# Two feed-forward norms of a two-block float32 kernel: 1/rms applied as a row on VectorE instead of a diagonal on TensorE

## What is computed

```python
# first block
x = x + gate1 * rmsnorm(y, g_post_mix[l])
h = rmsnorm(x, g_pre_ffn[l]) * (1.0 + scale2) + shift2      # "norm1"
gu = h @ w_ffn_in[l]
...
# second block
x = x + ... @ w_out[i]
h = rms_norm(x, norm_ffn_w[i])                                # "norm3"
u = causal_depthwise_conv(h @ w_ffn_up[i], ...)
...
x = x + g * (p[i] @ w_ple_proj[i])                            # p's projection
```

## Time and profile before

| what | us |
|---|---|
| median of three runs | 2794.21 (2787.49 to 2797.47) |
| the profiled execution, its own time | 2796.14 |
| its span in the trace | 2794.4 |
| TensorE busy | 2725.7 (98% of the span) |
| VectorE busy | 1820.3 (65%) |
| ScalarE busy | 1290.2 (46%) |
| GpSimd busy | 290.6 (10%) |
| mean granted TensorE clock | 0.991 of full |

### The profile page before, as it was taken

How to read it: one execution, slowest core, us unless ns; L and a number is a source line. 1 busy time by engine, 2 the same in 40 slices (tenths; PEclk the granted TensorE clock), 3 DMA queues, 4 the chain that set the end, 5 groups by cost and what they waited for, 6 DMA issues and landing times.

```text
span 2794.4 us, 38988 instructions
## 1 busy us (share of the span) xinstructions
PE 2725.7 (98%) x14835; PEld 2346.2 (84%) x14835; DVE 1820.3 (65%) x2017; ACT 1290.2 (46%) x1555; POOL 290.6 (10%) x161
## 2 busy tenths in 40 slices
PE   4899999999999999999999999999999999999998
PEld 4798888788888888888888989878888888888887
DVE  7966779689955556655567544656666654666555
ACT  2256554334444444444444444535555533555454
POOL 3010122100000100000100000100113110131100
PEclk8899999999999999999999999999999999999999
DMA  9975646698935567755566654445555565555553
GB/s 373 353 258 195 224 152 215 227 326 305 340 127 193 180 203 249 254 181 188 187 222 244 216 166 151 161 145 180 182 185 190 180 201 190 192 184 194 182 199 131
DMA packets 299522, 588.70 MB, mean 211 GB/s; under 512 B 12282, under 2 KB 19438, under 8 KB 298510
## 3 DMA queue, kind: packets, MB, share of 16 engines
q1 hardware_dynamic: 292816, 577.84, 61.0%
q10 hardware_dynamic: 6590, 9.27, 1.0%
HBM read 584.98 MB, written 2.10 MB: 210 GB/s over the span
## 4 chain that ended last, share of the span: by engine, by line
PE 89%; DVE 7%; issue 2%; ACT 1%; DMA 1%; SPq 0%; POOL 0%; DVEq 0%; POOLq 0%; ACTq 0%
PE psum L781 13%; PE psum L785 13%; PE psum L783 13%; PE bank L974 12%; PE psum L974 12%; PE bank L977 6%; PE psum L977 6%; PE psum L792 2%; PE psum L796 2%; PE psum L794 2%; DVE ada_acc L865 2%; DVE mod_acc L652 2%; DVE w_lo L739 2%; PE bank L2647 1%; PE bank L947 1%
## 5 line engine op out<-in xcount | busy, mean ns | idle before, releaser
L739 DVE TENSOR_TENSOR w_lo<-raw,w_hi 128x1024 fp32r<-128x1024 f32 x912 | 1165.3, 1293 | 836.7 <-ACT w_hi L727 825.7
L727 ACT ACTIVATE w_hi<-raw 128x1024 fp32r<-128x1024 f32 x912 | 953.6, 1054 | 1269.4 <-PE psum L785 568.4
L974 PE MATMUL psum<-h_both,w_hi 128*128 128x512 f32 x1408 | 495.1, 395 | 0.8 <-DVE x L2415 0.7
L974 PE MATMUL bank<-h_both,w_hi 128*128 128x512 f32 x1408 | 493.8, 395 | 0.0
L977 PE MATMUL bank<-h_both,w_lo 128*128 128x256 f32 x1408 | 394.8, 280 | 0.0
L977 PE MATMUL psum<-h_both,w_lo 128*128 128x256 f32 x1408 | 394.8, 280 | 0.0
L781 PE MATMUL psum<-w_hi,h_both 128*128 128x512 f32 x880 | 348.6, 396 | 0.8 <-ACT tokbuf L1826 0.7
L785 PE MATMUL psum<-w_hi,h_both 128*128 128x512 f32 x880 | 343.5, 390 | 0.0
L783 PE MATMUL psum<-w_lo,h_both 128*128 128x512 f32 x880 | 343.4, 390 | 0.0
L974 PEld LDWEIGHTS psum<-h_both,w_hi 128*128 128x128 f32 x1408 | 264.0, 187 | 62.7 <-DVE x L2415 1.0
L974 PEld LDWEIGHTS bank<-h_both,w_hi 128*128 128x128 f32 x1408 | 263.9, 187 | 61.9
(11 more groups left out here) (369 smaller groups left out, 3188.5 us busy)
## 6 DMA issues: line engine op xcount, KB each, us to landing
raw<-in_w_in_dram SPq DMA_DIRECT2D x120, 1024.0 KB, 5.2
raw<-in_w_ffn_in_dram SPq DMA_DIRECT2D x88, 1024.0 KB, 5.0
raw<-in_w_ffn_up_dram SPq DMA_DIRECT2D x88, 1024.0 KB, 5.0
raw<-in_w_ada_dram SPq DMA_DIRECT2D x64, 1024.0 KB, 5.2
raw<-in_w_ffn_out_dram SPq DMA_DIRECT2D x44, 1024.0 KB, 5.2
raw<-in_w_ffn_down_dram SPq DMA_DIRECT2D x44, 1024.0 KB, 5.1
ada_raw<-in_w_ada_dram SPq DMA_DIRECT2D x64, 512.0 KB, 8.0
raw<-in_w_out_dram SPq DMA_DIRECT2D x32, 1024.0 KB, 5.3
```

Source lines behind the costliest of these rows:

```text
L727: nc.scalar.activation(w_hi[:, slot, :, 0:ncol], raw[:, rs, 2 * h:2 * h + 2, 0:ncol], ACT.Copy).then_inc(split_hi, inc)
L739: nc.vector.tensor_tensor(w_lo[:, slot, :, 0:ncol], raw[:, rs, 2 * h:2 * h + 2, 0:ncol], w_hi[:, slot, :, 0:ncol].bitcast(F32), ALU.subtra ...
L974: pe.matmul(region[:, f, :].rearrange("p (s t) -> p s t", s=2), w_hi[:, slot, kk, cols_], h_both[:, :, k, :], start=first, stop=False, ski ...
```

## The change

1. `normed_dve` is no longer called in norm1, norm2 and norm3. A new `r_row_pe` waits for `rms` itself and multiplies the 1/rms column of `stats` (broadcast along its free axis as the stationary operand) with the identity; the result, a row of 1/rms on all partitions, lies in bank 3 (norm1, norm3) or bank 0 (norm2). VectorE copies it to `r_row`.
2. norm1 and norm3 transpose `x` as it is (L945's form). In norm1 VectorE writes `tmp = bank*gain*r_row`, ScalarE `h_hi = tmp + shift`, VectorE `h_lo = tmp + shift - h_hi`. In norm3 VectorE writes `tmp = bank*gain*r_row`, ScalarE `h_hi = tmp`, VectorE `h_lo = tmp - h_hi`.
3. norm1's first three pairs are transposed as the residual's columns get ready, with 18 unread matmuls in front and 14 behind; norm3's first three pairs are transposed in front of p's projection. The fourth pair follows the row in both, as it uses the same bank.
4. norm1: the weight half of VectorE's list (3 to 4) stands behind the residual and its sum instead of in front.
5. `keep_busy` writes to bank 3 instead of bank 0.

```diff
+        def r_row_pe(pe, stage, b, r):
+
+            pe.wait_ge(sem("rms"), r + 1)
+            pe.wait_ge(bank_free[b], fill(stage, b))
+            for t in range(TT):
+                mm = pe.matmul(bank[:, b, t * P:(t + 1) * P], stats[:, r, 2 + t:3 + t].to_broadcast([P, P]),
+                               ident[:], start=t == 0, stop=t == TT - 1, skip_group_check=True)
+            mm.then_inc(bank_full[b], 1)
+
+        def keep_busy(pe, ready, n):
+
+            pe.wait_ge(*ready)
+            for k in range(n):
+                pe.matmul(bank[:, 3, :].rearrange("p (s t) -> p s t", s=2), h_hi[:, k % KD, 0:P],
+                          h_both[:, :, k % KD, :], start=True, stop=True, skip_group_check=True)
...
@@ split_dve (norm3: row=r_row) @@
-                        ins = nc.vector.tensor_scalar(
-                            tmp[:, b % 2, k, :], bank[:, b % 4, k * TOK:(k + 1) * TOK],
-                            gain[:, f:f + 1], shift[:, f:f + 1], ALU.mult, ALU.add)
+                        tile_ = bank[:, b % 4, k * TOK:(k + 1) * TOK]
+                        if row is None:
+                            ins = nc.vector.tensor_scalar(tmp[:, b % 2, k, :], tile_, gain[:, f:f + 1],
+                                                          shift[:, f:f + 1], ALU.mult, ALU.add)
+                        else:
+                            ins = nc.vector.scalar_tensor_tensor(tmp[:, b % 2, k, :], tile_, gain[:, f:f + 1],
+                                                                 row[:], ALU.mult, ALU.mult)
...
@@ ScalarE, norm1 @@
-            split_act(act, "norm1", h_hi, KD, a_cols[:, 1, :], mod_cols[:, 3 * KD:4 * KD], between=plan.up1[0])
+            for b in range(KD // 2):
+                if b > 4:
+                    split_w_hi(act, plan.up1[0], 0, b - 1, b)
+                act.wait_ge(sem("norm1_scaled"), b + 1)
+                for k in range(2):
+                    f = 2 * b + k
+                    nc.scalar.activation(h_hi[:, f, :], tmp[:, b % 2, k, :], ACT.Identity,
+                                         bias=mod_cols[:, 3 * KD + f:3 * KD + f + 1]).then_inc(sem("norm1_hi"), 1)
+            split_w_hi(act, plan.up1[0], 0, 7, 8)
...
@@ VectorE, norm1 @@
-            split_w_lo(dve, plan.up1[0], 0, 3, 4)
             dve.wait_ge(sem("x_again"), 16)
             residual_dve(dve, chain, 1)
-            normed_dve(dve, 2)
-            split_dve(dve, "norm1", h_hi, h_lo, KD, a_cols[:, 1, :], mod_cols[:, 3 * KD:4 * KD], between=plan.up1[0])
+            split_w_lo(dve, plan.up1[0], 0, 3, 4)
+            dve.wait_ge(bank_full[3], filled("r_row1", 3))
+            nc.vector.tensor_copy(r_row[:], bank[:, 3, 0:TOK]).then_inc(bank_free[3], 1)
+            dve.wait_ge(bank_free[3], emptied("r_row1", 3))
+            def lower1(b):
+                dve.wait_ge(sem("norm1_hi"), 2 * b + 2)
+                for k in range(2):
+                    f = 2 * b + k
+                    ins = nc.vector.scalar_tensor_tensor(
+                        h_lo[:, f, :], tmp[:, b % 2, k, :], mod_cols[:, 3 * KD + f:3 * KD + f + 1],
+                        h_hi[:, f, :].bitcast(F32), ALU.add, ALU.subtract)
+                ins.then_inc(bank_free[b % 4], 1)
...
+                    ins = nc.vector.scalar_tensor_tensor(
+                        tmp[:, b % 2, k, :], bank[:, b % 4, k * TOK:(k + 1) * TOK], a_cols[:, 1, f:f + 1], r_row[:],
+                        ALU.mult, ALU.mult)
+                ins.then_inc(sem("norm1_scaled"), 1)
+                if b:
+                    lower1(b - 1)
+                if b > 4:
+                    split_w_lo(dve, plan.up1[0], 0, b - 1, b)
...
@@ TensorE, norm1 @@
-            keep_busy(pe, "norm1", 44)
-            pe.wait_ge(sem("normed"), 4)
-            normed_products(pe, plan.up1[0], "norm1", 2, up="up1_0")
+            keep_busy(pe, (bank_free[3], fill("r_row1", 3)), 18)
+            for b in range(3):
+                pe.wait_ge(sem("x_ready"), 2 * (b // 2 + 1))
+                transpose_pair_pe(pe, "norm1", x, b)
+            keep_busy(pe, (bank_free[3], fill("r_row1", 3)), 14)
+            r_row_pe(pe, "r_row1", 3, 2)
+            transpose_pair_pe(pe, "norm1", x, 3)
+            for h in range(KD // 2):
+                up_products(pe, plan.up1[0], 0, 0, "up1_0", ready="norm1", part=(h, h + 1))
+                if h < 4:
+                    transpose_pair_pe(pe, "norm1", x, 4 + h)
...
@@ norm2 @@
-            keep_busy(pe, "norm2", 20)
+            keep_busy(pe, (bank_free[3], fill("norm2", 3)), 20)
...
-                mm = pe.matmul(bank[:, 0, t * P:(t + 1) * P], ones[:], diag[:, t, :], start=t == 0,
-                               stop=t == TT - 1, skip_group_check=True)
-            mm.then_inc(bank_full[0], 1)
+            r_row_pe(pe, "r_row", 0, 4)
...
@@ TensorE, norm3 @@
+            for b in range(3):
+                pe.wait_ge(psum_free[ph.pair[b // 2]], ph.freed(0, b // 2))
+                transpose_pair_pe(pe, "norm3", x, b)
             tile_ready(pe, "ple", 0)
             proj_products(pe, 0)
-            pe.wait_ge(sem("normed"), 8)
-            normed_products(pe, plan.up2[0], "norm3", 5, up="up2_0")
+            r_row_pe(pe, "r_row3", 3, 5)
+            transpose_pair_pe(pe, "norm3", x, 3)
+            for h in range(KD // 2):
+                up_products(pe, plan.up2[0], 0, 0, "up2_0", ready="norm3", part=(h, h + 1))
+                if h < 4:
+                    transpose_pair_pe(pe, "norm3", x, 4 + h)
```

More of the change, by code:

```diff
@@ L343, in bank_uses @@
     uses += [
[L344 removed]
+        ("r_row1", (0, 0, 0, 1)), ("norm1", (2, 2, 2, 2)), ("up1_0", (FFN_PARTS[0][1],) * 4), ("mod_down0", (0, 0, 0, 2)),
         ("up1_1", (FFN_PARTS[1][1],) * 4), ("mod_down1", (0, 0, 0, 2)),
@@ L349, in bank_uses @@
     return uses + [
-        ("norm3", (2, 2, 2, 2)), ("up2_0", (FFN_PARTS[0][1],) * 4),
+        ("r_row3", (0, 0, 0, 1)), ("norm3", (2, 2, 2, 2)), ("up2_0", (FFN_PARTS[0][1],) * 4),
         ("up2_1", (FFN_PARTS[1][1],) * 4),
@@ L991, in up_products @@
                 half(idx, range(4))
-        def keep_busy(pe, stage, n):
-            pe.wait_ge(bank_free[0], fill(stage, 0))
-            for k in range(n):
-                pe.matmul(bank[:, 0, :].rearrange("p (s t) -> p s t", s=2), h_hi[:, k % KD, 0:P],
-                          h_both[:, :, k % KD, :], start=True, stop=True, skip_group_check=True)
         def normed_products(pe, ph, stage, r, transposed=False, up=None):
@@ L1052, in gained_pair_dve, with split_dve @@
             ins.then_inc(bank_free[b % 4], 1)
-        def split_dve(dve, stage, hi, lo, tiles, gain=None, shift=None, between=None, ahead=4):
+        def split_dve(dve, stage, hi, lo, tiles, gain=None, shift=None, row=None, between=None, ahead=4):
             def lower(b):
@@ L1060, in lower @@
                                         ).then_inc(bank_free[b % 4], 1)
-            if shift is not None:
+            if shift is not None or row is not None:
                 for b in range(tiles // 2):
@@ L1075, in split_dve @@
                         lower(b - 1)
-                    if between and b > 4:
+                    if between and b > ahead:
                         split_w_lo(dve, between, 0, b - 1, b)
@@ L1842, in _ @@
                 proj_act(0, j)
-            split_act(act, "norm3", h_hi, KD, gain_of("norm_ffn_w_2"), between=plan.up2[0], ahead=2)
+            split_act(act, "norm3", h_hi, KD, gain_of("norm_ffn_w_2"), shift=r_row, between=plan.up2[0], ahead=2)
             for part, (g0, n) in enumerate(FFN_PARTS):
@@ L2166, in _ @@
             part_sums_dve(dve, 1, part_sq[:, 0])
-            split_w_lo(dve, plan.up1[0], 0, 3, 4)
             dve.wait_ge(sem("x_again"), 16)
             residual_dve(dve, chain, 1)
-            normed_dve(dve, 2)
-            split_dve(dve, "norm1", h_hi, h_lo, KD, a_cols[:, 1, :], mod_cols[:, 3 * KD:4 * KD], between=plan.up1[0])
+            split_w_lo(dve, plan.up1[0], 0, 3, 4)
[10 more added lines that the diff above has]
+                ins.then_inc(bank_free[b % 4], 1)
+            for b in range(KD // 2):
+                dve.wait_ge(bank_full[b % 4], filled("norm1", b % 4, b // 4))
+                if b >= 2:
+                    dve.wait_ge(bank_free[(b - 2) % 4], emptied("norm1", (b - 2) % 4, (b - 2) // 4))
+                for k in range(2):
+                    f = 2 * b + k
+                    ins = nc.vector.scalar_tensor_tensor(
[6 more added lines that the diff above has]
+                    split_w_lo(dve, plan.up1[0], 0, b - 1, b)
+            lower1(KD // 2 - 1)
+            split_w_lo(dve, plan.up1[0], 0, 7, 8)
             for part, (g0, n) in enumerate(FFN_PARTS):
@@ L2254, in _ @@
                     if at == (0, 0):
-                        split_w_lo(dve, ph, 0, *span(ph, 0, part=(4, 6)))
-                        normed_dve(dve, 4)
-                        split_w_lo(dve, ph, 0, *span(ph, 0, part=(6, 8)))
+                        split_w_lo(dve, ph, 0, *span(ph, 0, part=(4, 8)))
```

(13 more changed lines are left out.)

1 line of the change is left out of this document (removed).

## The result

The change made the kernel slower: 2798.90 us (median of 20 runs, 2795.12 to 2804.64) against 2793.52 (20 runs, 2787.49 to 2800.78), 5.4 us more, a ratio of 1.0018 with a 95% interval of 1.0012 to 1.0024. The forecast was 3.4 us faster, and 2798.90 lies outside its range. The profiled execution took 2798.85 us, span 2797.1, against 2796.14.

The account below looks back on a forecast made before the run. The prediction took TensorE, busy for 98% of the span, to bound the kernel. Norm1 2.7 us plus norm3 0.7 us made 3.4 us faster: 2790.8 us against the median (2792.7 profiled), range 2785.5 to 2797.

Parts of the forecast that it names:

- The sum of the norms: Norm1 2.7 us faster plus norm3 0.7 us faster, 3.4 us in all; chance 0.43 as summed.
- the clock, taken at nothing: In norm3, TensorE's new idling was taken not to lower the clock; ends: nothing, or 1.5 us if it falls.
- Transposing x as it is: Norm1 and norm3: a pair takes 0.36 us against 0.80 by diag; four pairs save 1.8 us in each norm.
- norm1 up to the row: Residual starts 0.7 us earlier, second 1/rms at 771.8; unread matmuls end about 770.2 and delay nothing.
- VectorE's weight half: In norm1, moved behind the sum, it runs during GpSimd's 1/rms, ending at 771.9; later load costed at nothing.
- norm1 from the row on: Row, copy, multiplications, additions and low parts put the first product at 775.8 instead of 778.48, 2.7 us earlier.
- VectorE's rival: VectorE becomes the bound, row multiplications costing double L1095's; together 4.2 us slower, 2798.4; chance 0.04.
- The 15.4 and 18.1 us of the prediction's signs: Norm1's first product was to come 15.4 us behind the last product before the stop; before, 18.1.
- The clock in norm1: 1.2 GHz expected again, over norm1's first products, costing 1.8 us (ends: nothing and 2.3).
- norm3: First product 1.1 us later, against 1.8 us saved on four pairs: 0.7 us faster.
- the rival I gave 0.29: The clock falls in norm3 too, costing 1.5 us: 1.9 us faster in all, 2792.3; chance 0.29.

Follow-up runs that it names:

- early: Changed kernel with norm1's weight half moved behind the third pair and norm3's row made inside p's projection; 2797.31 us, a single run.
- n1_only: The change without its part in norm3, which is as in the kernel before; 2794.65 us, ratio to before 1.0008.
- before_grouped: Kernel before with each k-tile's four 512-column up matmuls first, then the four of 256, instead of alternating; 2794.92 us, ratio 1.0013.
- n3_grouped: The change without its part in norm1, up matmuls of 512 columns first, then 256; 2795.72 us, ratio to before in its old order 1.0018.
- before_nudge: Kernel before with one unread two-column matmul ahead of every up group; 2806.33 us, ratio 1.0052.
- n3_only: The change without its part in norm1, which is as in the kernel before; 2796.14 us, ratio to before 1.0021.

## Why the prediction was wrong, point by point

- **The step that failed** first is one that was not written: the sum ends at the norms and takes every product outside them at its old pace, a term put at nothing without a reason. The pace of the up products behind the two norms is no constant of the kernel. 22 of 44 groups were slow before, 32 after, 10 x 0.427 = 4.3 us.
- **The sum of the norms failed too**, by its own terms: 3.4 us faster was forecast, and the two norms' stretches give 1.49 faster and 1.42 slower, together 0.1. In norm3 the clock, taken at nothing, cost 1.8 us and the start 0.3 more than forecast; in norm1 the start came 1.2 later than forecast. For the two profiled executions the account closes: forecast 3.4 faster, measured 2.7 slower, 6.1 apart, which is 4.3 of rhythm, 2.1 in norm3 and 1.2 in norm1, less 1.5 for the start of the span (0.6), norm2 (0.8) and the end (0.1).
- Over the 20 runs only totals are known, so how the 5.4 us of the medians divide is not read from them; but in the order with one rhythm 1.0 of it is left. That the changed kernel draws more slow stages than the kernel before, run after run, is what the totals suggest and not what a count shows. I had seen the spread of 10 us in three runs and used it as noise; it was, for the most part, a cause with states of its own.
- **Transposing x as it is**: right. Four records of L945 and 0.35 us for the pair at 781.23; nothing of this went wrong.
- **norm1 up to the row**: the residual started at once behind the first 1/rms (763.11), the unread matmuls ended in time. Its 1/rms came 0.9 late, because GpSimd's step took 1.10 beside VectorE's weight half, which I had costed at nothing; `early` shows both the cause and the 0.9.
- **norm1 from the row on**: 772.18 to 776.44 is 4.3 us, forecast 4.0. L2211 took what L1095 did, 0.48 an instruction, so VectorE's rival fell; L2199 takes 0.48 too. (The 15.4 and 18.1 us of the prediction's signs are counted from the first unread matmul, not from the last product.)
- **The clock in norm1**: it fell, as forecast, over the first products, and the price was about right: the first half of product and the pair behind it took 5.14 us against a forecast 2.8 + 0.36 + 1.8 = 5.0. From the first product to the second group it was 26.10 us before and 26.06 after: the 1.8 of the four pairs went to the clock, as the sum had it. The length was underrated: 6.8 us of 1.2 GHz, and 10.2 in `n1_only`, where that half took 5.68. What I had not seen is that the fall in the kernel before was not certain either: `before_grouped` and `n3_grouped` have norm1 as before up to its first product, and no fall, and that product comes at 16.65 us, not 18.12; `before_nudge` and `n3_only` fell as before. Against a kernel whose clock holds there, the change gains nothing in norm1.
- **norm3**: the first product was 10.91 us behind the mixer's last against 9.47, 1.4 later, forecast 1.1. The clock fell, the rival I gave 0.29, at a price of 1.5: from the first product to the second group it was 25.91 us before and 25.89 after, so the fall took the 1.8 of the four pairs. It is the less usual case, two profiles of ten. Where the clock held, in `n3_only`, the stretch gained 0.3 against 0.7.
- Of the rivals, none named the pace of the products. VectorE's, at 2798.4 the nearest in number, had the right sign by luck and the wrong place.

Not settled: what in an entry picks the rhythm. A small matmul ahead of a group can, but neither 2 nor 128 columns led to one rhythm everywhere. Nor is it known why 18 of the changed kernel's 20 runs lie within 2797.69 to 2799.71, when its relatives with one part or one small matmul changed are spread over 9 to 14 us. And the clock's fall in a stop is read here, not explained: nothing tells beforehand in which execution it comes.

## What to carry to other kernels

When a long run of identical matmuls fills most of a span, count them per microsecond in the middle of each stage, in both profiles, before reading the edited place: here 0.007 us on a pair outweighed all that the edit did. A kernel whose runs spread more than its edits are worth should be compared in a form that has one rhythm (matmuls of one width next to each other), even if that form is not the fastest (here it is 3 us slower). And keep a long VectorE instruction like this weight half from lying across a GpSimd step on the path (0.9 us here); in a stop like norm1's, spread a few unread matmuls up to its very end.

## What was unexpected of the hardware

- Two steady rhythms of TensorE at the same granted clock, 346.7 and 353.3 ns for a float32r matmul of 512 columns and one of 256 with different weights, kept through ten or more groups and turned by a single matmul (two of four tries). Where all matmuls have 512 columns (L781 to L785 of the kernel before), they start 227 ns apart. The Trainium skill, "TensorE: Matmul & The Clock Gate", section "Wait — 56ns, not 53.3ns?", gives N / 2.4 GHz + 2.5 ns start to start for back-to-back matmuls; an estimate by it is 215.8 + 109.2 = 325 ns for the pair. The trace, in which every matmul has a weight load of its own, disagrees in either rhythm, and the measurement decides.
- Four of 512 and four of 256 in groups run at 22.43 us a group, slower than the fast alternation (22.19) and faster than the slow one (22.61).
- An unread matmul of 2 columns ahead of a group starts 0.03 us before the first product and still lengthens the group by 0.11 us.
- GpSimd's tensor_scalar on two columns: 1.09 or 1.10 us with VectorE's 1024-column subtraction across it (eleven profiles), 0.19 without (nine). In the changed kernel it ends at 771.35, VectorE's instruction at 771.30.
- The stay at 1.2 GHz behind similar stops was 0, 3.4, 6.8 or 10.2 us in different profiles. With norm1 as before it was 3.4 in three profiles and 0 in the two in groups; with the changed norm1 6.8 in seven and 10.2 in three; with the changed norm3 0 in eight and 3.4 in two.
